# Low operand parts displaced by 64 to 384 bytes from the high parts in a split-precision kernel

## The reference

```
# first block, layer 0: pooling mixer; layer 1: attention; both then the MLP
y = pool_mixer(h, w_pool, pool_scale)            # layer 0
o = attention(h @ w_qkv);  y = o @ w_o           # layer 1: "qkv", "o"
a = relu(h @ w_up)                               # "up0", "up1": 1024 -> 4096
x = x + g2 * ((a * a) @ w_down)                  # "down0", "down1": 4096 -> 1024
# second block
z = h @ w_in + b_in                              # "glu", "rx", "rg", "gb", "ga"
r, i = sigmoid(blocks(xb, wa)), sigmoid(blocks(xb, wx))   # "gates"
y_a, y_b = u @ conv_w_out, (hb * gelu(z_rg)) @ lru_w_out  # "conv", "lru"
x = x + (sigmoid(z_ga) * y_a + sigmoid(z_gb) * y_b) @ w_mix_out   # "mix"
x = x + (silu(h @ w1) * (h @ w3)) @ w2           # "ffn", then "w2": 2816 -> 1024
```

## Time and profile before

| | us |
|---|---|
| median of three runs | 1011.12 |
| the profiled execution, its own time | 1013.9 |
| its span, first to last instruction | 1012.1 |
| TensorE busy with matmuls | 977.0 |
| VectorE busy | 788.2 |
| ScalarE busy | 560.6 |
| GpSimd busy | 105.1 |

### The profile page before, as it was taken

One profiled execution on the slowest core, in us unless ns is written; L12 is line 12 of the kernel. 1 busy time (PEld: TensorE's weight loads), 2 busy tenths in 40 slices (PEclk: granted clock), 3 DMA queues, 4 the chain that ended last, 5 costly groups with the idle time before them and its releaser, 6 DMA issues.

```text
span 1012.1 us, 19319 instructions
## 1 busy us (share of the span) xinstructions
PE 977.0 (97%) x7468; PEld 910.6 (90%) x7468; DVE 788.2 (78%) x1370; ACT 560.6 (55%) x922; POOL 105.1 (10%) x134
## 2 busy tenths in 40 slices
PE   4799999999999999999999999999999999999996
PEld 2479998888989899999888999998889999999996
DVE  4757986999777677667876899999998887777554
ACT  3248675444655567776544666677126564444352
POOL 0000000000000000000000000999910000000000
PEclk8799999999999999999999999999999999999998
DMA  9998798887564865554555455453446555555531
GB/s 378 421 419 336 275 378 300 318 325 280 144 203 115 307 239 177 189 186 167 208 179 213 164 193 170 164 208 127 165 139 221 182 187 189 194 179 190 193 116 42
DMA packets 35880, 222.27 MB, mean 220 GB/s; under 512 B 3883, under 2 KB 9180, under 8 KB 9436
## 3 DMA queue, kind: packets, MB, share of 16 engines
q1 hardware_dynamic: 35804, 221.22, 60.6%
HBM read 220.13 MB, written 1.07 MB: 219 GB/s over the span
## 4 chain that ended last, share of the span: by engine, by line
PE 81%; DVE 8%; DMA 4%; ACT 4%; issue 2%; DVEq 0%; SPq 0%; ACTq 0%
PE bank L656 22%; PE bank L645 17%; PE bank L646 16%; PE bank L650 12%; PE bank L982 5%; PE bank L1035 3%; DMA mod_raw<-w_mod 2%; DVE w_lo L1472 2%; PE s_banks L679 1%; ACT w_hi L1109 1%; DVE s_banks L1879 1%; DVE bank L1854 1%; PE s_banks L1035 1%; DMA raw<-weights 1%; DVE ab L1847 1%
## 5 line engine op out<-in xcount | busy, mean ns | idle before, releaser
L1472 DVE TENSOR_TENSOR w_lo<-raw,w_hi 128x1024 fp32r<-128x1024 f32 x284 | 346.3, 1225 | 32.1 <-ACT w_hi L1109 29.7
L1109 ACT ACTIVATE w_hi<-raw 128x1024 fp32r<-128x1024 f32 x284 | 296.1, 1050 | 93.6 <-PE bank L656 89.9
L645 PE MATMUL bank<-xg_hi,w_hi 128*128 128x258 f32 (+1 forms) x1376 | 340.9, 285 | 0.8 <-ACT w_hi L1109 0.5
L646 PE MATMUL bank<-xg_lo,w_hi 128*128 128x258 f32 (+1 forms) x1376 | 336.5, 281 | 0.0
L645 PEld LDWEIGHTS bank<-xg_hi,w_hi 128*128 128x128 f32 x1376 | 259.7, 189 | 5.8 <-issue 4.7
L646 PEld LDWEIGHTS bank<-xg_lo,w_hi 128*128 128x128 f32 x1376 | 260.1, 189 | 0.2
L656 PE MATMUL bank<-xg_hi,w_lo 128*128 128x258 f32 (+1 forms) x1376 | 198.3, 282 | 0.3 <-DVE w_lo L1472 0.3
L656 PEld LDWEIGHTS bank<-xg_hi,w_lo 128*128 128x128 f32 x1376 | 178.5, 189 | 0.8 <-DVE w_lo L1472 0.5
L650 PE MATMUL bank<-hid,w_hi 128*128 128x512 f32 x512 | 127.7, 391 | 0.0
L650 PEld LDWEIGHTS bank<-hid,w_hi 128*128 128x128 f32 x512 | 91.5, 188 | 15.8
L656 PEld LDWEIGHTS bank<-hid,w_lo 128*128 128x128 f32 x512 | 68.5, 188 | 5.3
(11 more groups left out here) (245 smaller groups left out, 1262.0 us busy)
## 6 DMA issues: line engine op xcount, KB each, us to landing
raw<-weights SPq DMA_DIRECT2D x157, 1024.0 KB, 4.9
mod_raw<-w_mod SPq DMA_DIRECT2D x28, 1024.0 KB, 11.4
mod_raw<-w_dots SPq DMA_DIRECT2D x20, 1024.0 KB, 9.6
toep<-bias_by_distance SPq DMA_DIRECT2D x8, 256.0 KB, 5.4
x<-x_in SPq DMA_DIRECT2D x1, 1024.0 KB, 4.9
toep<-bias_by_distance SPq DMA_DIRECT2D x8, 128.0 KB, 3.9
y_out<-yout SPq DMA_DIRECT2D x4, 256.0 KB, 2.4
c_all<-c_row SPq DMA_DIRECT2D x1, 512.0 KB, 14.8
```

What stands on the lines that cost most here:

```text
L645: pe.matmul(dst, hi, r_hi, start=start, stop=False, skip_group_check=True)
L646: pe.matmul(dst, hi, r_lo, start=False, stop=False, skip_group_check=True)
L1109: act.activation(pool_w_hi[:, at, :] if name == "pool" and at < 2 else w_hi[:, at % HL, :], raw[:, slot, (at % 2) * UT * P:(at % 2 + 1) * ...
L1472: ve.tensor_tensor(lo, raw[:, slot, (at % 2) * UT * P:(at % 2 + 1) * UT * P], hi.bitcast(F32), ALU.subtract).then_inc(lo_done, 1)
```

## The change

A new function `two_parts` allocates the high and the low part in one tensor. Ahead of them lie the same 64 bytes as before. Behind the high part, and again behind the low one, are `apart` unused values of four bytes. The high parts keep their addresses; the low ones move by 128 bytes in `hid` (down0, down1), 64 in `o`, 384 in `act` (gates, mix) and 256 in `f` (w2). `behind_a2`, the filler that keeps the buffers behind `act` clear of it, grows by 768 bytes, and all that lies behind it (`u`, `y`, `grg`, `rt`, `ig`, `av`, `sga`, `sgb`, `pool_prod`, `h32`) moves by as much; `yout` moves by 512 bytes. Each engine executes the same operations in the same order; apart from tile names only a few register instructions that compute addresses in two of VectorE's loops are packed differently.

```diff
+        def two_parts(name, count, apart, where):
+            n = count * SEQ
+            both = where.enter_context(nc.sbuf_tensor(name, [P, HALF + 2 * (n + apart)], F32R, align_bytes=LINE))
+            both = both[:, HALF:].rearrange("p (h n) -> p h n", h=2)
+            return both, *(both[:, h, 0:n].rearrange("p (c n) -> p c n", n=SEQ) for h in range(2))
...
-            half_line("hid", part)
-            hid = sb("hid", [P, 2, FFC, SEQ], F32R, part)
-            hid_hi, hid_lo = hid[:, 0], hid[:, 1]
+            hid, hid_hi, hid_lo = two_parts("hid", FFC, 32, part)
...
-            half_line("o", part)
-            o_hi = sb("o_hi", [P, DC, SEQ], F32R, part)
-            o_lo = sb("o_lo", [P, DC, SEQ], F32R, part)
+            _, o_hi, o_lo = two_parts("o", DC, 16, part)
...
-                half_line("act", inner)
-                act_hi = sb("act_hi", [P, RC, SEQ], F32R, inner)
-                act_lo = sb("act_lo", [P, RC, SEQ], F32R, inner)
+                _, act_hi, act_lo = two_parts("act", RC, 96, inner)
             a2 = sb("a2", [P, RC, SEQ], F32, part)
-            sb("behind_a2", [P, RC * SEQ + 2 * HALF], F32, part)
+            sb("behind_a2", [P, RC * SEQ + 2 * HALF + 2 * 96], F32, part)
...
-            half_line("f", part)
-            f_hi = sb("f_hi", [P, F2C, SEQ], F32R, part)
-            f_lo = sb("f_lo", [P, F2C, SEQ], F32R, part)
+            _, f_hi, f_lo = two_parts("f", F2C, 64, part)
...
-                    by_high_once(dst[:, :], (U0[name] + j) % HL, s, hid[:, :, k, :], k == 0)
+                    by_high_once(dst[:, :], (U0[name] + j) % HL, s, hid[:, :, k * SEQ:(k + 1) * SEQ], k == 0)
```

## The result

The changed kernel took 1016.33 us in the median of 18 runs (1013.99 to 1019.16), the kernel before 1012.32 us in 18 runs of its own (1010.01 to 1015.95). The medians lie 4.0 us apart, which is a quotient of 1.0040. The ratio estimated together with its 95% interval is 1.0048 (1.0039 to 1.0056), or 4.9 us. It is not the quotient of the medians, and how the two estimates come apart is not known; both are given where it matters. Either way the kernel is slower. The prediction said 1010.3 us and 1004.5 to 1015.5. The sign was wrong and the time lies 0.8 us above the range. Two later timings of the same kernel gave ratios of 1.0031 (1.0019 to 1.0043) and 1.0040 (1.0024 to 1.0055), with medians 3.9 and 3.3 us apart.

A forecast was written before the change was run, and what follows sets the result against it. TensorE's matmul spacing was taken to bound the touched phases. Terms 0 (down projections) - 1.2 (w2) + 0.4 (mix) - 0.2 (gates) + 0.2 (o) = -0.8 us on the median 1011.12 gave 1010.3 us, range 1004.5 to 1015.5.

The forecast's parts named there:

- I take 0: Down projections, hid 128 bytes further: rhythms already take turns at their mean, so 0, within -3.1 to +3.7 us.
- The rival of the collision: Down projections, mix and other touched phases: staggered matmuls of both parts collide, +7.0 us, 1018.1 us; chance 0.15.
- deciding point of 231 ns: Down projections: the collision rival decides once the spacing of 512-column matmuls exceeds 231 ns.
- w2, -1.2 us: w2, f 256 bytes further: rhythm drawn anew from all slow, half of the possible -2.4 us gain taken.
- the third rival: All touched phases: entry into a phase alone sets the rhythm, addresses do nothing; 0, so 1011.1 us; chance 0.10.
- mix and gates, +0.4 and -0.2: mix and gates, act 384 bytes further: rhythms drawn anew, half fast and half slow, +0.4 and -0.2 us.
- o, +0.2 us: o, low part 64 bytes further: between +0.4 all slow and -0.3 all fast; possible 0.3 more for lying on 128 bytes.
- Moved buffers and registers, 0: Buffers moved by 768 bytes and VectorE register instructions: costed at nothing, registers covered by VectorE's waits for TensorE.
- the prediction's own base: Whole kernel: the median before of 1011.12 us, on which the sum of -0.8 us was set.
- The stagger makes matmuls of both parts collide: Down projections, mix, gates, o and w2: slower by +3.7, +0.9, +0.1, +0.7 and +1.6, in all +7.0 us; chance 0.15.
- Addresses do nothing: All touched phases: rhythm set only by how a phase is entered; 0, so 1011.1 us; chance 0.10.
- the first rival: Down projections, w2, gates, o: the new distance locks streams in the fast rhythm, -6.3 us, 1004.8 us; chance 0.25.

The follow-up runs named there:

- e2_f256: Changed kernel with hid, o and act back at 0, only the low part of f 256 bytes further; ratio to the kernel before 1.0001 (0.9988 to 1.0014).
- e4_apart0: Changed kernel with the new function but hid, o, act and f all at distance 0; ratio to the kernel before 1.0001 (0.9988 to 1.0013).
- e3_act384_o64: Changed kernel with hid and f back at 0, keeping act at 384 and o at 64 bytes; ratio to the kernel before 1.0006 (0.9991 to 1.0020).
- xg_even: Kernel before, with xg from glu on in chunks 1024 bytes apart and its low part 9216 bytes from the high; 1006.06 us against 1012.69, ratio 0.9930.

## Why the prediction was wrong

**What bounds the kernel.** Right. TensorE is busy throughout in down0, mix and w2, each changed spacing came out one to one in the phase, and no other engine's work in the phases changed.

**Down projections, "I take 0".** This is the step that failed. Measured +1.12 and +1.15 us, +2.3 in all, inside the bounds of -3.1 and +3.7. The argument was that the rhythms took turns and so stood at their mean, to be drawn anew. But these phases are not drawn at all. At 0 and 256 bytes the turns came out the same in all ten profiles (88.15 to 88.16 and 88.12 to 88.13 us), and at 128 bytes, in all five profiles that have it, the short matmuls, which read only the unmoved high part, do not find the fast rhythm any more (64 groups at 0.94 instead of half of them at 0.91, +1.0 us in both phases), and the long ones go from 229.0 to 231.4 ns (+1.2 us). The rival of the collision had the direction and the place right, and its deciding point of 231 ns was just passed. Two units took 5.58 us, close to the mark of 5.60 that the prediction had set for it.

**w2, -1.2 us.** Wrong in its reason. I took one profile's slow w2 for a property of the kernel. It was the outcome of one execution: f at 0 and at 256 bytes give 59.84 or 62.15 us alike, and e2_f256 timed 1.0001. The term should have been 0. For this phase the third rival had it right: at these two distances the entry decides, and the address does not.

**mix and gates, +0.4 and -0.2.** Mix measured +0.44, but not by a draw of half its units: each unit at 384 bytes takes 2.77 us, as mixtures of spacings from 113 to 119 ns. Gates at uneven places (the low part not a multiple of 256 bytes from the high one) took 19.11 to 19.17 us in all four kernels that have them; at even places 18.64 to 19.23 with a mean of 18.9. So +0.2, not -0.2, though the even ones reach past it.

**o, +0.2 us.** Measured 26.02 to 26.06 at uneven places against a mean of 25.7 (25.40 to 26.00) at even ones: +0.3. No cost of its own shows for the low part at 64 bytes, which comes to lie on a multiple of 128: 64, 128 and 384 bytes are alike in o.

**Moved buffers and registers, 0.** Right as far as the runs tell (e4_apart0, and gb, ga and lru in e3_act384_o64).

**The sum and the base.** The corrected terms are 2.3 + 0.4 + 0.2 + 0.3 + 0 = 3.3 us (as 2.27, 0.44, 0.25 and 0.35 before rounding). The three timings gave 4.9, 3.1 and 4.0 us by their ratios, of which the first's interval (3.9 to 5.7) does not hold 3.3, and 4.0, 3.9 and 3.3 us by their medians. So 0.4 us (medians) to 0.7 us (ratios) of the mean are not assigned. No touched phase shows them, the opening may hold them, and this stays open. The measured 1016.33 us is 6.0 above the forecast: 0.8 for the gain that did not come, 4.0 between the medians, and 1.2 because the median of before was 1011.12 us in the three runs that the prediction had and is 1012.32 in 18. The corrected sum on the prediction's own base is 1014.4 us, inside its range. That the measured time lies outside it is thus in part the base; that the sign is wrong is not.

**The rivals.** "The stagger makes matmuls of both parts collide" came nearest, forecast with 0.15 and +7.0 us: it was right in its direction and in the down projections and mix as the places. A collision itself was not shown. What it set too high was w2, where 256 bytes proved to be no stagger at all (+1.6 forecast, 0 measured), the long matmuls (+2.6 forecast, +1.2 measured), and mix and o at about double. "Addresses do nothing", and with it the single spacing of the Trainium skill ("TensorE: Matmul & The Clock Gate", section "Back-to-back issue gap": 262 cycles, 109 ns, for 256 columns), does not describe this stream: the same matmuls took 113.3 to 118 ns on average, by the place of their operands and by the draw, and no phase came down to 109. The Trainium skill gives that number for an isolated matmul, not for a stream with a weight load for each. The slow `xg`, which I held against the first rival and then did not use, was the best witness: the prediction said that it does not show what the distance alone would do, and xg_even showed that with even places ffn falls from 117.5 to the 113.3 ns of the fast rhythm.

## What to carry to other kernels

Matmuls on 32-bit split operands with 256 columns run fastest, here, when all moving operands of a phase start at the same place within 256 bytes. Mix and w2 then fall into one of two rhythms, 4% apart, at their entry (2.72 or 2.83 us a unit). At uneven places the fast one never appeared in them; their units took 2.77 to 2.84 us. So compare several profiles before a phase's time is taken for a property of the kernel, and weigh a small change per phase (first to last matmul) rather than by the total: single runs of one kernel lay up to 6 us apart here, which hid all but the largest effects. Where one buffer is laid out differently and slower by a few per cent of a matmul's spacing, as `xg` was, it is worth a run: it was 0.5 to 0.7% of the time.

## What the runs showed of the hardware

- The spacing depends on distance with a period of 256 bytes: down0 88.16, 89.79, 89.27, 89.48 and again 88.16 us at 0, 64, 128, 192 and 256 bytes, and mix 21.67, 22.22, 22.10, 21.67 and 22.10 at 0, 64, 128, 256 and 384. No mechanism for it was shown. The addresses of the weights and of the high parts were the same in all these runs, so it is the place of the low part that counts, against the high part or against the weights. No run moved both parts together to tell these apart. The sizes of the buffers in the kernel speak for the high part: counted from the weights, `act_hi` and `f_hi` lie 128 bytes apart within 256, and both mix and w2 reach 2.72 us a unit with the low part at the place of their own high part, while mix does not with it 128 bytes on, at the place of `f`.
- The time of a unit comes in whole steps of 6.67 ns (16 cycles at the full clock of 2.4 GHz): 2.720 us is 408 of them, 2.820 is 423, and 28.27 us for ten units of w2 is 4240. A unit of w2 at 192 bytes takes 2.840 us, which is 426. In down0 of before it is the pair of units in turn that does, 5.513 us or 827 steps. It is as if a repeating stream had to close on a raster of 16 cycles; no run tests this.
- Two executions with the same addresses part behind a break of 0.20 us that both have, and each keeps its rhythm for the 500 matmuls that follow. What tips it there is not shown.
